# Seven block products in place of eight in a feed-forward block, and down projections in thirds

## The chip, the cores and the metric

The kernel runs on one core of one Trainium2 chip. The metric is the device time of one execution in microseconds (us): the median of 3 timed runs. A profile is of one further execution. TensorE (PE) multiplies, VectorE (DVE), ScalarE (ACT) and GpSimd (POOL) work elementwise, SyncE (SP) issues transfers. SBUF is the on-chip memory, PSUM the eight banks that PE writes to.

## The reference

Two layers of an encoder trunk, all in float32, for 512 prompt frames and 8 x 16 sample frames, 640 rows of 1024 together. A layer is

```
h = h + 0.5 * rmsnorm(swiglu(rmsnorm(h, g0), f1g, f1u, f1d), g1)
h = h + rmsnorm(mixer(rmsnorm(h, g2)), g3)
h = h + 0.5 * rmsnorm(swiglu(rmsnorm(h, g4), f2g, f2u, f2d), g5)
swiglu(x, wg, wu, wd) = (silu(x @ wg) * (x @ wu)) @ wd      # 1024 -> 2816 -> 1024
```

The mixer (pooling, sliding-window attention, a short convolution, three gates and an output projection) is not part of the change.

## The kernel before

Everything is transposed: features lie on the 128 partitions and frames along the free dimension, in two halves of `HT` = 320 frames. 1024 features are `KD` = 8 tiles, 2816 hidden features `NF` = 22 tiles. A float32 operand is split into a high part (rounded to float32r) and a low part (the rest), and each product is made in three passes, high x high, high x low, low x high, so one k-tile costs three matmuls of 128 x 128 by 320.

A *group* (`group`, line 529) is one output tile of 128 features by 320 frames in one PSUM bank: 24 matmuls with 8 k-tiles. A *pair* is two weight columns of 128 (slots 0 and 1) by two halves: four groups in banks 0 to 3. For a gate/up pair the two slots are the gate and the up column of one hidden tile f, so f costs 4 x 24 = 96 matmuls. SP loads the weights of a slot into `raw` in four transfers. ACT rounds them to `w_hi`, and DVE subtracts to get `w_lo` (both called `stage`, lines 851 and 1158). PE waits for `w_split` (weights ready) and `evac` (bank free), the second four groups back.

A feed-forward block (FFN), `ffn` on each engine, runs twice a layer, four times in all. It has two halves fg. Each has `FG` = 11 gate/up tiles, then the down projection over these 11 hidden tiles (four pairs, 33 matmuls a group); the second half adds to `y_ffn`. For each gate/up half-tile DVE takes `scaled` and `up` from PSUM times `inv_x` (line 1279), ACT applies silu, DVE multiplies to `mid` (line 1286), ACT rounds `mid_hi`, and POOL subtracts for `mid_lo` (line 1615). Before the first down group PE waits for `mid_split`:

```
pe.wait_ge(mid_split, unit + 2 * FG - 1)
...
for q in range(4):
    if q == 2:
        pe.wait_ge(mid_split, unit + 2 * FG)
```

A *seam* joins two blocks. While PE makes the last eight down groups (`last_four`) and the first eight groups of the next block (`first_four`, 2 weight pairs), the other engines finish the norm of the old block, update `h`, and make `x_hi`, `x_lo` of the next: squares on ACT, their sums on POOL (`add_square`, line 1577), column sums and spreading on PE (`sums`, `spread`), root on ACT, reciprocal and `new_h`, `x_low` on DVE. The order of the squares is written out in `SEAM_SQ` (behind an FFN) and `SEAM_SQ_MIX` (behind a mixer), and `first_four` places the sums differently behind a mixer. In the first tiles (`hidden_four`) the takes wait for `inv_x`.

The order of each engine is written by hand. Loops over layers, tiles and pairs run on the engines (`Fori`).

Of the kernel before, what the change touches and what calls it, by code (L numbers as in the profile page):

```python
# [8 lines left out]
F32R = mybir.dt.float32r  # L28
# [3 lines left out]
ds = bass.ds  # L32

P = 128
# [9 lines left out]
FG = NF // 2  # L44
# [12 lines left out]
FFN_PAIRS = 2 * (FG + KD // 2)  # L57
# [21 lines left out]
DVE_STEPS = 3 * 20 + 4 * ATT_STEPS + 5 + 2 * KD  # L79
POOL_STEPS = 3 * 4 + 3 + 8 + 2 + 6  # L80
# [7 lines left out]
           ("x", 5), ("y", 14), ("x", 6), ("x", 7), ("y", 15)]  # L88
SEAM_SQ_MIX = SEAM_SQ[:13] + [("y", 15), ("x", 6), ("x", 7)]


def trunk_kernel(nc, x_prompt, x_sample, state_pool, state_conv, cache_k, cache_v, norm_g, ffn1_w_gate,
# [5 lines left out]
    with ctx:  # L98
# [16 lines left out]
        at_h, at_x, at_mid, at_y = take(KD * TB), take(2 * KD * TB), take(24 * TB), take(KD * TB)  # L115
# [4 lines left out]
        mid_hi = view("mid_hi", FG * NT, at_mid, F32R)  # L120
        mid_lo = view("mid_lo", FG * NT, at_mid + FG * TB, F32R)
        br_hi = view("br_hi", KD * NT, at_mid, F32R)
        br_lo = view("br_lo", KD * NT, at_mid + KD * TB, F32R)
        mg_lo = view("mg_lo", KD * NT, at_mid + 2 * KD * TB, F32R)
        rows = view("rows", 5 * D, at_mid)
        in_mid = [at_mid + 2 * KD * TB]

        def in_mg(name, cols):
# [7 lines left out]
        assert in_mid[0] <= at_mid + 3 * KD * TB  # L136
        y_ffn = view("y_ffn", KD * NT, at_y)
        mg_hi = view("mg_hi", KD * NT, at_y, F32R)
# [6 lines left out]
        raw = [own(f"raw{s}", FG * P) for s in range(2)]  # L145
        w_hi = [own(f"w_hi{s}", FG * P, F32R) for s in range(2)]
        w_lo = [own(f"w_lo{s}", FG * P, F32R) for s in range(2)]

        W8 = 4 * KD * P
        w_first, w_out_last = (
            [[view(f"{n}_{part}{s}", KD * P, at_mid + off + W8 * (2 * s + i), F32R) for s in range(2)]
             for i, part in enumerate(("hi", "lo"))]
            for n, off in (("w_first", 16 * TB - 8 * W8), ("w_out_last", 16 * TB - 4 * W8)))
        assert 16 * TB - 8 * W8 >= 2 * TB and 8 * P <= 4 * 2 * P

        at_tmp = take(8 * 4 * HT + 256)
        scaled = [view(f"scaled{s}", HT, at_tmp + 4 * HT * s) for s in range(2)]
        silu = [view(f"silu{s}", HT, at_tmp + 4 * HT * (2 + s)) for s in range(2)]  # L160
        up = [view(f"up{s}", HT, at_tmp + 4 * HT * (4 + s)) for s in range(2)]
        mid = [view(f"mid{s}", HT, at_tmp + 4 * HT * (6 + s)) for s in range(2)]
        w_tail = view("w_tail", 4 * (FG - KD) * P, at_tmp, F32R)
        sig = [view(f"sig{s}", HT, at_tmp + 4 * HT * (2 + s)) for s in range(6)]
        PB = 4 * (WIN + 1) + 4
        prob = [view(f"prob{s}", PB, at_tmp + 4 * PB * s) for s in range(3)]
        prob_t = [view(f"prob_t{s}", 4 * P, at_tmp + 12 * PB + 16 * P * s) for s in range(2)]
        assert 12 * PB + 32 * P <= 8 * 4 * HT + 256

        at_seam = take(12 * 4 * HT)  # L170
        sq, diag, low, acc_y, acc_x, tb = (
            [view(f"{n}{s}", HT, at_seam + 4 * HT * (2 * i + s)) for s in range(2)]
            for i, n in enumerate(("sq", "diag", "low", "acc_y", "acc_x", "tb")))
        tb.append(own("tb2", HT))
        v_win = view("v_win", 8 * P, at_seam)
        win_v = view("win_v", PE_W, at_seam + 32 * P)
        assert 32 * P + 4 * PE_W <= 6 * 4 * HT
        inv_x = [own(f"inv_x{s}", HT) for s in range(2)]
        xv = [own(f"xv{s}", HT) for s in range(2)]
        k_s = own("k_s", DEC_B * KEYS_S)  # L180
        at_vs = take(4 * DEC_B * P)
        v_s = view("v_s", DEC_B * P, at_vs)
        pc_out = view("pc_out", 8 * P, at_vs)
        at_kr = take(16 * P)
        k_raw = view("k_raw", 4 * P, at_kr)
        prm_rows = view("prm_rows", DEPTH * P, at_kr)
        at_sr = take(4 * (PW + CW))
        sp_raw, sc_raw = view("sp_raw", PW, at_sr), view("sc_raw", CW, at_sr + 4 * PW)
        new_rows = view("new_rows", 4 * P, at_sr)
        kv_out = own("kv_out", 3 * P)  # L190
        wp = own("wp", DEPTH * 2 * P)
        wp_now = own("wp_now", 2 * P)
# [8 lines left out]
        eps1, eps4 = own("eps1", 1), own("eps4", 1)  # L201
# [16 lines left out]
        mid_made = sem("mid_made")  # L218
        mid_hi_made = sem("mid_hi_made")
# [78 lines left out]
        def w_cols(part, where, s, nk):  # L298


            if where == "main":
                return [(0, nk, (w_hi, w_lo)[part][s][:, 0:nk * P])]
            if where in ("first", "out_last"):
                return [(0, nk, (w_first if where == "first" else w_out_last)[part][s][:, 0:nk * P])]
            over_x = (x_hi, x_lo)[part][:, 4 * s * NT:4 * (s + 1) * NT].rearrange("p (k t) -> p k t", t=NT)
            o = (2 * s + part) * (FG - KD) * P
            return [(0, KD, over_x[:, :, HT:HT + 2 * P]), (KD, nk, w_tail[:, o:o + (nk - KD) * P])]

        def w_tile(part, where, s, k):
            if where == "x":  # L310
                if k < KD:
                    at = (4 * s + k // 2) * NT + HT + (k % 2) * P
                    return (x_hi, x_lo)[part][:, at:at + P]
                o = ((2 * s + part) * (FG - KD) + k - KD) * P
                return w_tail[:, o:o + P]
            return {"main": (w_hi, w_lo), "first": w_first, "out_last": w_out_last}[where][part][s][:, k * P:(k + 1) * P]

        def raw_cols(s, a, z, like):
            r = raw[s][:, a * P:z * P]
            return r.rearrange("p (k c) -> p k c", c=2 * P) if len(like.shape) == 3 else r  # L320
# [66 lines left out]
        def _(sp):  # L387
# [12 lines left out]
            def columns(w, l, row0, nk, col, slot):  # L400

                src = w[ds(l, 1)].rearrange("a (k p) c -> p (a k) c", p=P)[:, row0 // P:row0 // P + nk, :]
                dst = raw[slot][:, 0:nk * P].rearrange("p (k c) -> p k c", c=P)
                q = (nk + LOADS - 1) // LOADS
                return [(dst[:, a:min(a + q, nk)], src[:, a:min(a + q, nk), ds(col, P)]) for a in range(0, nk, q)]
# [27 lines left out]

            def ffn(n, l, first):
                for g in range(2):
                    pair = l * PAIRS + FFN_PAIR0[n] + (FG + KD // 2) * g

                    with sp.Fori(2 if first and g == 0 else 0, FG) as f:
                        gate_up(pair + f, n, l, f + g * FG)
                    with sp.Fori(0, KD // 2) as i:  # L440
                        for s in range(2):
                            load(pair + FG + i, s, columns(w_ffn[n][2], l, g * FG * P, FG, (2 * i + s) * P, s))
# [10 lines left out]
            with sp.Fori(0, DEPTH) as l:  # L453
# [62 lines left out]
        def _(pe):  # L516
# [28 lines left out]
            K8, KF = range(KD), range(FG)  # L545
# [5 lines left out]
            def first_four(pair, g, n, after_mixer):  # L551
# [5 lines left out]
                def stand(at):  # L557

                    if at == ((0, "lo", 0, 0) if after_mixer else (0, "hi", 1, 1)):
                        sums(acc_y[1], BY[1], sq0 + (22 if after_mixer else 24))  # L560
                    if at == ((0, "lo", 1, 2) if after_mixer else (0, "hi", 1, 4)):
                        sums(acc_x[0], BX[0], sq0 + 24)
                    if at == ((0, "all", 2, 0) if after_mixer else (0, "lo", 0, 1)):
                        spread(BY[1], 4 * n + 1)
                    if at == ((0, "all", 2, 4) if after_mixer else (0, "lo", 1, 0)):
                        spread(BX[0], 4 * n + 2)
# [1180 lines left out]
```

## Time and profile before

| | |
|---|---|
| median of the timed runs | 2792.03 us (2791.22 to 2793.0) |
| span of the profiled execution | 2795.9 us |
| mean granted clock of TensorE | 0.991 |
| busy PE, DVE, ACT, POOL | 2757.9, 1245.5, 849.1, 447.1 us |
| moved by transfers | 208.44 MB, mean 75 GB/s |

The span runs from the first to the last instruction of the profiled execution and is 3.9 us above the median of the timed runs. A busy time counts an engine's instructions; PE's matmuls are pipelined, so one lasts longer (0.31 us) than the distance to the next. A granted clock of 1.00 is 2.4 GHz, 0.50 is 1.2 GHz.

### The profile page before, as it was taken

How to read it: one execution, taken by the hardware profiler on the slowest of the kernel's cores; microseconds unless marked ns; L12 is line 12 of the kernel's file. 1: busy time of each engine (PE TensorE's matmuls, PEld its weight loads, DVE VectorE, ACT ScalarE, POOL GpSimd, SP SyncE). 2: the span in 40 equal slices, each digit the busy share in tenths (PEclk: the TensorE clock that was granted, in tenths of full speed). 3: DMA queues.
4: the chain of work that ended last, by engine and by line, in shares of the span. 5: the costliest groups of instructions: out<-in, count | busy, mean ns of one | idle time of the engine just before them, and what ended most of it. 6: DMA issues, size and time to landing. Idle time of an engine off the chain costs nothing.

```text
span 2795.9 us, 54256 instructions
## 1 busy us (share of the span) xinstructions
PE 2757.9 (99%) x18682; PEld 2719.4 (97%) x18682; DVE 1245.5 (45%) x1997; ACT 849.1 (30%) x1331; POOL 447.1 (16%) x473
## 2 busy tenths in 40 slices
PE   8999999999999999999999999999999999999998
PEld 8999999989999999999999999999899999999997
DVE  5332333674444733233453333355644455333335
ACT  4221223333333522122332122233333343212223
POOL 3100112240001410011321001132300032100112
PEclk9999999999999999999999999999999999999998
DMA  3232222122223222222222222221122222222222
GB/s 104 75 90 86 73 82 71 48 61 66 74 73 91 59 73 81 66 75 87 65 70 75 83 83 75 86 73 50 46 75 75 77 76 61 75 83 76 74 79 89
DMA packets 425146, 208.44 MB, mean 75 GB/s; under 512 B 42425, under 2 KB 423323, under 8 KB 424987
## 3 DMA queue, kind: packets, MB, share of 16 engines
q1 hardware_dynamic: 421956, 203.46, 25.3%
q10 hardware_dynamic: 3062, 3.38, 0.4%
q8 instruction: 68, 1.11, 0.2%
q14 instruction: 60, 0.48, 0.1%
HBM read 203.28 MB, written 5.29 MB: 75 GB/s over the span
## 4 chain that ended last, share of the span: by engine, by line
PE 94%; DVE 3%; issue 1%; ACT 0%; POOL 0%; DVEq 0%; DMA 0%; SPq 0%; ACTq 0%; POOLq 0%
PE ps L540 30%; PE ps L541 29%; PE ps L542 29%; DVE h L1198 1%; DVE x_lo L1180 1%; PE ps L593 1%; PE ps L641 1%; PE ps L588 1%; PE ps L589 1%; PE ps L663 1%; PE ps L521 1%; DVE w_lo L1162 0%; PE ps L527 0%; POOL acc_y L1580 0%; PE ps L691 0%
## 5 line engine op out<-in xcount | busy, mean ns | idle before, releaser
L540 PE MATMUL ps<-x_hi,w_hi 128*128 128x320 f32 x3648 | 1136.6, 312 | 0.0
L542 PE MATMUL ps<-x_hi,w_lo 128*128 128x320 f32 x3648 | 1127.2, 309 | 0.0
L541 PE MATMUL ps<-x_lo,w_hi 128*128 128x320 f32 x3648 | 1127.0, 309 | 0.0
L540 PEld LDWEIGHTS ps<-x_hi,w_hi 128*128 128x128 f32 x3648 | 684.8, 188 | 11.4 <-issue 6.5
L541 PEld LDWEIGHTS ps<-x_lo,w_hi 128*128 128x128 f32 x3648 | 685.0, 188 | 0.2
L542 PEld LDWEIGHTS ps<-x_hi,w_lo 128*128 128x128 f32 x3648 | 684.8, 188 | 0.0
L858 ACT ACTIVATE w_hi<-raw 128x1024 fp32r<-128x1024 f32 (+1 forms) x326 | 362.3, 1114 | 758.8 <-PE ps L542 758.8
L1162 DVE TENSOR_TENSOR w_lo<-raw,w_hi 128x1024 fp32r<-128x1024 f32 (+1 forms) x326 | 423.4, 1300 | 179.9 <-ACT w_hi L858 179.9
L540 PE MATMUL ps<-mid_hi,w_hi 128*128 128x320 f32 x1232 | 382.0, 310 | 0.0
L541 PE MATMUL ps<-mid_lo,w_hi 128*128 128x320 f32 x1232 | 380.7, 309 | 0.0
L542 PE MATMUL ps<-mid_hi,w_lo 128*128 128x320 f32 x1232 | 380.7, 309 | 0.0
L1615 POOL TENSOR_TENSOR mid_lo<-mid,mid_hi 128x320 f32 x160 | 141.1, 882 | 1297.6 <-ACT mid_hi L948 677.3
L1279 DVE TENSOR_TENSOR up<-ps,inv_x 128x320 f32<-128x320 f32 x176 | 86.3, 490 | 332.7 <-PE ps L542 332.7
L541 PEld LDWEIGHTS ps<-mid_lo,w_hi 128*128 128x128 f32 x1232 | 231.3, 188 | 0.3
L540 PEld LDWEIGHTS ps<-mid_hi,w_hi 128*128 128x128 f32 x1232 | 231.3, 188 | 0.3
L1580 POOL TENSOR_TENSOR acc_y<-acc_y,sq 128x320 f32<-128x320 f32 x96 | 113.3, 1180 | 739.5 <-ACT sq L869 739.2
L542 PEld LDWEIGHTS ps<-mid_hi,w_lo 128*128 128x128 f32 x1232 | 231.3, 188 | 0.0
L1279 DVE TENSOR_TENSOR scaled<-ps,inv_x 128x320 f32<-128x320 f32 x176 | 86.3, 490 | 247.3 <-PE ps L542 247.3
L948 ACT ACTIVATE mid_hi<-mid 128x320 f32 (+1 forms) x80 | 37.8, 472 | 316.9 <-DVE mid L1286 316.9
L1208 DVE COPY y_ffn<-ps 128x320 f32 (+1 forms) x64 | 31.5, 492 | 200.8 <-PE ps L542 200.8
L1337 DVE TENSOR_TENSOR scaled<-ps,inv_x 128x320 f32<-128x320 f32 x96 | 47.1, 491 | 163.5 <-PE ps L542 163.5
L1580 POOL TENSOR_TENSOR acc_x<-acc_x,sq 128x320 f32<-128x320 f32 x104 | 103.1, 991 | 91.6 <-ACT sq L869 72.8
(199 smaller groups left out, 3001.1 us busy)
## 6 DMA issues: line engine op xcount, KB each, us to landing
raw<-in_ffn_w_gate_dram SPq DMA_DIRECT2D x360, 128.0 KB, 2.2
raw<-in_ffn_w_up_dram SPq DMA_DIRECT2D x360, 128.0 KB, 2.3
raw<-in_w_in_dram SPq DMA_DIRECT2D x304, 128.0 KB, 2.2
raw<-in_ffn_w_down_dram SPq DMA_DIRECT2D x192, 192.0 KB, 2.7
raw<-in_ffn_w_down_dram SPq DMA_DIRECT2D x64, 128.0 KB, 2.8
raw<-in_w_branch_dram SPq DMA_DIRECT2D x64, 128.0 KB, 2.6
raw<-in_w_out_dram SPq DMA_DIRECT2D x64, 128.0 KB, 2.3
rows<-in_x_prompt_dram SPq DMA_DIRECT2D x4, 512.0 KB, 5.3
```

Source lines behind the costliest of these rows:

```text
L521: mm = pe.matmul(ps[0:SP_, b, c:c + 1], acc[:, c * SP_:(c + 1) * SP_], ones[:, 0:1], start=True, stop=True)
L540: pe.matmul(bank(b), wh, tile(xh, k, hf), start=k == ks[0], stop=False)
L541: pe.matmul(bank(b), wh, tile(xl, k, hf), start=False, stop=False)
L542: mm = pe.matmul(bank(b), wl, tile(xh, k, hf), start=False, stop=k == ks[-1])
L858: ins = act.activation(dst, raw_cols(s, a, z, dst), ACT.Copy)
L948: act.activation(at_tile(mid_hi, f, 0), mid[0][:, :], ACT.Copy).then_inc(mid_hi_made, 1)
L1162: ins = dve.tensor_tensor(lo, raw_cols(s, a, z, lo), f32(hi), ALU.subtract)
L1208: dve.tensor_copy(dst, bank(q)).then_inc(evac, 1)
L1279: dve.tensor_tensor(dst[:, :], bank(b), inv_x[hf][:, :], ALU.mult).then_inc(evac, 1)
L1337: return dve.tensor_tensor(dst, cut(bank(b), cols, bb), cut(inv_x[hf], cols, bb), ALU.mult)
L1580: pool.tensor_tensor(acc[:, :], acc[:, :], sq[pos % 2][:, :], ALU.add).then_inc(sq_added, 1)
L1615: pool.tensor_tensor(at_tile(mid_lo, f, hf), mid[hf][:, :], f32(at_tile(mid_hi, f, hf)), ALU.subtract).then_inc(mid_split, 1)
```

## The change

Of the 22 hidden tiles of an FFN the first 3 are made as before. The other 19 are made in runs of 3, 8 and 8 (`RUNS`), each run followed by a down projection over 6, 8 and 8 hidden tiles (`KT`).

For such a tile the four blocks of the activations (two halves of frames by two halves of four k-tiles) and the four blocks of the weights (two halves of k-tiles by gate and up) form a 2 x 2 product. It is made by Strassen's method in Winograd's form: 7 products of 4 k-tiles (`product`, 12 matmuls each) in place of 8. Needed beside them are four sums of weight blocks per tile (`sum_b`, 128 x 512 each, DVE), a high and a low part of seven weight blocks (`hi` on ACT, `low` on DVE, 128 x 512 each, in a ring of seven slots), four sums of activation blocks once an FFN (`so_sum`, `so_split`, `so_low`, 16 instructions of 128 x 320 each), and sums of the products in PSUM (DVE, 7 reads of PSUM a tile; ACT copies the first product to `p1s`). The low part of the hidden tile moves from POOL to DVE for these tiles. A tile's weights come in eight transfers (`pair_load`) into one of two buffers, one of which shares its place with `raw`.

```diff
@@ constants @@
-FG = NF // 2
+KT = (6, 8, 8)
+RUNS = ((3, 3), (6, 8), (14, 8))
+PRODUCTS, EVACS, SUMS_B = 7, 9, 4
...
@@ constants @@
-           ("x", 5), ("y", 14), ("x", 6), ("x", 7), ("y", 15)]
-SEAM_SQ_MIX = SEAM_SQ[:13] + [("y", 15), ("x", 6), ("x", 7)]
+           ("x", 5), ("y", 14), ("y", 15), ("x", 6), ("x", 7)]
...
@@ tensor: product @@
+            def product(S, i, b, x):
+                pe.wait_ge(s_split, PRODUCTS * S + i + 1)
+                for k in range(4):
+                    wh, wl = ring_w(i, 0, k), ring_w(i, 1, k)
+                    xh, xl = x(0, k), x(1, k)
+                    pe.matmul(bank(b), wh, xh, start=k == 0, stop=False)
+                    pe.matmul(bank(b), wh, xl, start=False, stop=False)
+                    mm = pe.matmul(bank(b), wl, xh, start=False, stop=k == 3)
+                mm.then_inc(s_prod, 1)
...
@@ tensor: strassen @@
+                product(S, 0, bank_free(0), lambda p, k: tile(xs[p], k, 0))
+                sums_ready(4)
+                product(S, 1, bank_free(1), lambda p, k: so_tile(sos[p], 0, k))
+                product(S, 2, bank_free(2), lambda p, k: tile(xs[p], 4 + k, 0))
+                sums_ready(S_OPS)
+                product(S, 3, bank_free(3), lambda p, k: tile(xs[p], k, 1))
+                product(S, 4, bank_free(4), lambda p, k: so_tile(sos[p], 1, k))
+                product(S, 5, bank_free(5), lambda p, k: tile(xs[p], 4 + k, 1))
+                product(S, 6, bank_free(6), lambda p, k: so_tile(sos[p], 2, k))
...
@@ tensor: ffn, before a down projection @@
+                    pe.wait_ge(mid_split, unit - 2)
+                    for q in range(4):
+                        pe.wait_ge(s_evac, EVACS * (S1 + 2) + TAKEN_BY[PRODUCTS - 4 + q])
+                        alone(pe)
+                        group(pd, gd + q, q % 2, q, (mid_hi, mid_lo), ks, q // 2, last_mid if q == 0 else None)
...
@@ scalar: ffn, per Strassen tile @@
+                        act.activation(p1s[:, :], bank(product_bank(t, PRODUCTS * r)), ACT.Copy).then_inc(p1_taken, 1)
+                        if r:
+                            strassen_mid(S - 1, f - 1, ft - 1, 0)
+                        if more:
+                            hi(S + 1, t, r + 1, 0)
+                            hi(S + 1, t, r + 1, 1)
+                        strassen_silu(S, 0)
+                        if more:
+                            for i in range(2, 6):
+                                hi(S + 1, t, r + 1, i)
+                            strassen_silu(S, 1)
+                            strassen_mid(S, f, ft, 1)
+                            hi(S + 1, t, r + 1, 6)
+                        else:
...
@@ vector: ffn, the three ordinary tiles @@
+                scale(scaled[0], 0, 0, g0)
+                scale(scaled[1], 2, 0, g0 + 2)
+                so_sum(0)
+                multiply(0, 1, g0 + 1)
+                multiply(1, 3, g0 + 3)
+                so_sum(1)
+                second_half(sm - 1)
+                scale(scaled[0], FIRST_BANKS[0], 1, g0 + 4)
+                stage(p0 + 2, 0, KD)
+                multiply(2, FIRST_BANKS[1], g0 + 5)
+                stage(p0 + 2, 1, KD)
+                so_sum(2)
+                so_sum(3)
+                so_low(0, 2)
+                scale(scaled[1], 2, 1, g0 + 6)
+                multiply(3, 3, g0 + 7)
+                so_low(1, 1)
+                S0 = s_base(l, n, 0)
+                front(S0, 0, 0)
+                scale(scaled[0], 0, 0, g0 + 8)
+                front(S0, 0, 1)
+                multiply(4, 1, g0 + 9)
+                so_low(2, 3)
+                front(S0, 0, 2)
+                scale(scaled[1], 2, 1, g0 + 10)
+                multiply(5, 3, g0 + 11)
+                so_low(3, 0)
...
@@ vector: ffn, per Strassen tile, behind two weight sums @@
+                        dve.tensor_tensor(p_u2[:, :], made(1), p1s[:, :], ALU.add).then_inc(s_evac, 1)
+                        if more:
+                            low(S + 1, r + 1, 0)
+                        dve.tensor_tensor(scaled[0][:, :], made(2), p1s[:, :], ALU.add).then_inc(s_evac, 1)
+                        if more:
+                            sum_b(S + 1, t, r + 1, 2)
+                        dve.wait_ge(s_evac, taken + 2)
+                        dve.tensor_tensor(scaled[0][:, :], scaled[0][:, :], inv_x[0][:, :], ALU.mult).then_inc(s_evac, 1)
+                        dve.wait_ge(s_evac, taken + 1)
+                        dve.tensor_tensor(p_u3[:, :], made(3), p_u2[:, :], ALU.add).then_inc(s_evac, 1)
+                        if more:
+                            low(S + 1, r + 1, 1)
...
@@ vector: ffn, last tile of a run @@
+                            stage(pd, 0, KT[t])
+                        dve.tensor_tensor(p_u2[:, :], made(6), p_u2[:, :], ALU.add).then_inc(s_evac, 1)
...
@@ vector: ffn, behind the last tile of a run @@
+                    stage(pd, 1, KT[t])
+                    mid_low(S, ft, 1)
+                    mid_low(S, ft, 0)
...
@@ tensor, and so on every engine @@
-            with pe.Fori(0, DEPTH) as l:
+            for l in range(DEPTH):
```

In the three ordinary tiles the up half is multiplied straight out of PSUM (`multiply`), without the scaling by `inv_x`. To allow this, POOL puts the norm's factor into the sum of squares behind the block (`begin(..., True)`). All seams use one order, the former one behind a mixer. The loop over the layers is written out on every engine.

## Rows read from the trace of the kernel before

**Rows 1.** The page's first part: busy us, share of the span, instructions.
```profile
PE 2757.9 (99%) x18682; PEld 2719.4 (97%) x18682; DVE 1245.5 (45%) x1997; ACT 849.1 (30%) x1331; POOL 447.1 (16%) x473
```
**Rows 2.** The page's chain that ended last, by engine.
```profile
PE 94%; DVE 3%; issue 1%; ACT 0%; POOL 0%; DVEq 0%; DMA 0%; SPq 0%; ACTq 0%; POOLq 0%
```
**Rows 3.** Windows: us, busy PE, PEld, DVE, ACT, POOL (x), clock, DMA, GB/s.
```profile
60.00:230.00 170.00, 170.00 (x1161) 170.00 (x1160) 59.65 (x86) 41.71 (x59) 16.75 (x19) 1.00 0.28 81
```
**Rows 4.** Timeline of DVE, a gate/up tile: start, us, instruction [idle before].
```profile
152.22 0.49 DVE L1279 TENSOR_TENSOR scaled<-ps,inv_x 128x320 f32<-128x320 f32 x1 [2.28 <-PE ps L542]
...
156.83 1.23 DVE L1162 TENSOR_TENSOR w_lo<-raw,w_hi 128x1024 fp32r<-128x1024 f32 x1 [0.60 <-ACT w_hi L858]
157.97 0.48 DVE L1286 TENSOR_TENSOR mid<-silu,up 128x320 f32<-128x320 f32 x1
...
166.30 0.49 DVE L1279 TENSOR_TENSOR scaled<-ps,inv_x 128x320 f32<-128x320 f32 x1 [2.27 <-PE ps L542]
```
**Rows 5.** Timeline of DVE, first takes of the FFN behind a mixer.
```profile
950.32 0.48 DVE L1279 TENSOR_TENSOR scaled<-ps,inv_x 128x320 f32<-128x320 f32 x1
950.72 0.48 DVE L1279 TENSOR_TENSOR up<-ps,inv_x 128x320 f32<-128x320 f32 x1
```
**Rows 6.** Groups by line and form on ACT: count, busy us, mean ns, idle before.
```profile
L858 ACT ACTIVATE w_hi<-raw 128x1024 fp32r<-128x1024 f32 x270 | 285.0, 1058 | 490.3 <-PE ps L542 490.3
...
L948 ACT ACTIVATE mid_hi<-mid 128x320 f32 x72 | 34.0, 472 | 286.3 <-DVE mid L1286 286.3
```
**Rows 7.** Timeline of SP, four transfers of a weight slot.
```profile
70.36 2.06 SPq L398 DMA_DIRECT2D raw<-in_ffn_w_gate_dram  x4
```
**Rows 8.** The page's DMA issues: count, KB each, us to landing.
```profile
raw<-in_ffn_w_gate_dram SPq DMA_DIRECT2D x360, 128.0 KB, 2.2
```
**Rows 9.** Timeline of DVE, low parts of activations in two seams.
```profile
944.15 5.64 DVE L1180 SCALAR_TENSOR_TENSOR x_lo<-h,prm,x_hi 128x320 fp32r<-128x320 f32 x8
...
1405.65 1.47 DVE L1180 SCALAR_TENSOR_TENSOR x_lo<-h,prm,x_hi 128x320 fp32r<-128x320 f32 x3
```
**Rows 10.** Timeline of POOL beside the first of these; beside the second it has none.
```profile
938.60 8.53 POOL L1580 TENSOR_TENSOR acc_x<-acc_x,sq 128x320 f32<-128x320 f32 x8 [8.73 <-ACT sq L869]
```
**Rows 11.** Timeline of ACT, first silu of the FFN behind a mixer.
```profile
953.05 0.47 ACT L962 ACTIVATE silu<-scaled 128x320 f32<-128x320 f32 x1
```
**Rows 12.** Timeline of DVE, takes at two seams, mixer to FFN and FFN to FFN.
```profile
908.09 0.49 DVE L1208 COPY y_mix<-ps 128x320 f32<-128x320 f32 x1 [3.03 <-PE ps L542]
...
962.75 0.49 DVE L1279 TENSOR_TENSOR scaled<-ps,inv_x 128x320 f32<-128x320 f32 x1 [0.58 <-PE ps L542]
...
1376.44 0.49 DVE L1206 TENSOR_TENSOR y_ffn<-ps,y_ffn 128x320 f32<-128x320 f32 x1 [4.35 <-PE ps L542]
...
1436.84 0.49 DVE L1279 TENSOR_TENSOR scaled<-ps,inv_x 128x320 f32<-128x320 f32 x1 [0.56 <-PE ps L542]
```
**Rows 13.** Timeline of PE in the seam from FFN to mixer.
```profile
500.48 1.23 PE L521 MATMUL ps<-ones,acc_y 128*80 128x1 f32 x8 [2.66 <-POOL acc_y L1580]
```
**Rows 14.** Windows in two seams, columns as in rows 3.
```profile
499.00:500.00 1.00, 0.00 (x0) 0.00 (x0) 0.66 (x2) 1.00 (x2) 0.44 (x1) 0.94 0.36 81
500.00:501.00 1.00, 0.52 (x4) 0.53 (x5) 0.62 (x1) 0.35 (x1) 0.42 (x1) 0.50 0.00 0
...
510.00:511.00 1.00, 1.00 (x6) 0.81 (x6) 0.97 (x3) 0.30 (x1) 0.00 (x0) 0.94 0.00 0
...
924.00:928.00 4.00, 2.28 (x14) 1.76 (x13) 4.00 (x6) 2.52 (x6) 3.36 (x4) 1.00 0.16 47
```
**Rows 15.** Timeline of PE in the seam from mixer to FFN.
```profile
925.93 0.41 PE L588 MATMUL ps<-x_hi,w_hi 128*128 128x320 f32 x1 [0.58 <-ACT x_hi L876]
...
927.62 0.41 PE L588 MATMUL ps<-x_hi,w_hi 128*128 128x320 f32 x1 [1.14 <-ACT x_hi L876]
```
**Rows 16.** Timeline of DVE: last up take, first down take of an FFN.
```profile
183.90 0.49 DVE L1279 TENSOR_TENSOR up<-ps,inv_x 128x320 f32<-128x320 f32 x1 [0.48 <-PE ps L542]
...
188.87 0.49 DVE L1208 COPY y_ffn<-ps 128x320 f32 x1 [1.53 <-PE ps L542]
```

More of the change, by code:

```diff
@@ L154, in trunk_kernel @@
+        assert 2 * TB + 3 * W8 <= 8 * TB
+        w_out_last, w_x = (
+            [[view(f"{n}_{part}{s}", KD * P, at + W8 * (2 * s + i), F32R) for s in range(2)]
              for i, part in enumerate(("hi", "lo"))]
[L155 to L158 removed]
+            for n, at in (("w_out_last", at_mid + 16 * TB - 4 * W8), ("w_x", at_s)))
@@ L165, in trunk_kernel @@
+        sig = [view(f"sig{s}", HT, at_tmp + 4 * HT * (2 + s) if s < 4 else at_free + 4 * HT * (s - 4)) for s in range(6)]
         PB = 4 * (WIN + 1) + 4
         prob = [view(f"prob{s}", PB, at_tmp + 4 * PB * s) for s in range(3)]
[L167 to L171, printed above, removed]
+        assert 12 * PB <= 6 * 4 * HT
@@ L309, in w_tile, with w_of @@
-        def w_tile(part, where, s, k):
[L310 to L320, printed above, removed]
+        def w_of(part, where, s):
+            return {"main": (w_hi, w_lo), "first": w_first, "out_last": w_out_last, "x": w_x}[where][part][s]
@@ new lines, in ffn @@
+                for k in range(4):
+                    act.wait_ge(h_ready, 16 * (sm + 1))
+                    alone(act)
+                    act.activation(so_tile(so_raw, 0, k), tile(h, 4 + k, 1), ACT.Copy,
+                                   scale=gcol(l, 4 * n, 4 + k)).then_inc(xgb_made, 1)
+                roots(BX[1], sm - 1, 3, False)
+                silu_of(0, 1)
+                silu_of(1, 2)
+                keep_inv_x(1, sm - 1)
+                mid_hi_of(0, 0, 0, 3)
+                mid_hi_of(1, 1, 0, 4)
@@ L1135, in _ @@
             roots(BX[0], -1, 2, False)
-            with act.Fori(0, DEPTH) as l:
+            for l in range(DEPTH):
                 ffn(0, l, 3 * l, l, 2)
@@ L1559, in _ @@
             inverse(-1, 2)
-            with dve.Fori(0, DEPTH) as l:
-                own_.loop(l, DVE_STEPS)
+            for l in range(DEPTH):
                 ffn(0, l, 3 * l, l, 2)
@@ L1700, in _ @@
                 add_square(acc_x[0], 0, 16 + j)
-            with pool.Fori(0, DEPTH) as l:
-                own_.loop(l, POOL_STEPS)
+            for l in range(DEPTH):
                 ffn(0, l, 3 * l)
```

631 lines of the change are left out of this document (410 added, 221 removed).

## The prediction

> **What bounds the kernel now.** I read the page's busy times first, then its chain, then one stretch by windows, then single instructions in the timeline. TensorE (PE) is busy for 99% of the span, VectorE, ScalarE and GpSimd for less than half of it [rows 1], and the chain that ended last is 94% PE [rows 2]. In the stretch from 60 to 230 us, all gate/up and down projection, PE has no idle time, its granted clock is 1.00 (2.4 GHz), and 1161 matmuls take 170 us, 146.4 ns each [rows 3]. The same period comes out of the loop: the take of one group recurs after 166.30 - 152.22 = 14.08 us for 96 matmuls, 146.7 ns each [rows 4]. Group boundaries are inside both figures, so a boundary costs nothing visible. A time that falls must come from fewer matmuls, and the question is what PE then waits for.
>
> **What it removes.** A tile of hidden columns is now eight block products of 4 k-tiles by 3 passes, 96 matmuls; as a Strassen tile it is seven, 84. 19 of 22 tiles of each feed-forward block (FFN) change, and there are four FFNs: 12 x 19 x 4 = 912 matmuls. The down projections keep theirs (16 groups x 22 tiles x 3, cut 6 + 8 + 8 instead of 11 + 11). 912 x 146.7 ns = **-133.8 us**. Products of 12 matmuls double the boundaries; at the boundary cost of rows 3 and 4 that is nothing.
>
> **The Strassen step, per tile.** PE needs 84 x 146.7 ns = 12.32 us, 1.76 a product. VectorE (DVE) gets a new load. Per tile it issues four weight sums and seven low parts of 128x512, seven reads of PSUM at 128x320, and six more at 128x320 (two scalings, two hidden products, two hidden low parts): 11 wide and 13 narrow. The trace has no 512-wide instruction of this kind, so its spacing lies between neighbours: narrow ones without a wait start 0.40 us apart although each lasts 0.48 [rows 5], and a 1024-wide one is followed after 157.97 - 156.83 = 1.14 us although it lasts 1.23 [rows 4]. On the line between them 512 costs 0.60. So DVE needs 11 x 0.60 + 13 x 0.40 = 11.8 us of 12.32, 96%. From above: if spacing were the whole duration (0.48; 0.69 on the line to 1.23), 11 x 0.69 + 13 x 0.48 = 13.8. From below a lighter DVE gives PE nothing, since PE bounds then. I take 11.8, since rows 4 and 5 are the same instruction shapes, and cost the step at PE's 12.32. The cover is thin, but a late DVE doesn't stop PE at once: the next tile's weights are split during this one, and a bank comes round after eight products. The dependent pairs have another instruction between them, which fills the result's latency. ScalarE (ACT) has seven roundings of 512, one copy, two silus and two roundings of 320; 1024 takes it 1.06 us and 320 takes 0.47 [rows 6], so 512 some 0.63: 7 x 0.63 + 5 x 0.47 = 6.8 us, half of the step. Its in-order waits could add to DVE's 11.8, which is a rival below.
>
> The Trainium skill, VectorE: DVE Perf Modes, section "The DRAIN you can't avoid", says that after each DVE instruction the pipe is flushed and the next cannot start before it is empty. Read as a spacing of the whole duration that speaks against this change, and it is the slower rival below; the trace's 0.40 after a 0.48 us instruction doesn't bear it out so far.
>
> Weight traffic stays 1 MB a tile in eight DMAs. Four are issued in 2.06 us [rows 7] and land after 2.2 [rows 8], so eight are in after about 2 x 2.1 + 2.2 = 6.4 us. A buffer comes free some 3 us into one step and is wanted 3 us into the next: 12 us. Hidden; if the cover were gone, the excess over 12 would be paid at each tile.
>
> GpSimd (POOL) loses the hidden low parts but for six a FFN. DVE's three-operand instructions take 5.64 us for eight while POOL adds squares and 1.47 for three when it doesn't [rows 9, 10], some 0.7 against 0.47 from one to the next, so DVE also runs undisturbed in the Strassen steps. I use undisturbed spacings there.
>
> **Entry into Strassen, once a FFN.** The three ordinary tiles now carry the sums of the activations: on DVE 12 sums at 0.47, 4 at 0.40, 16 low parts at 0.40, 12 takes and products at 0.40, two weight splits at 1.14, four weight sums and four lows at 0.60 up to the fourth product: 25.5 us. In the FFN after the mixer DVE is free for it at 950.3 [rows 5]. Added to it are round trips through ACT, which follow in order: silu before the first product (its table load ends at 953.05 [rows 11]), the rounding of the sums behind the rounding of the hidden tile, the silu of the third tile behind three weight roundings that themselves wait for a DVE sum. Laid out instruction by instruction they and POOL's interference cost DVE some 7.7 us. So the fourth product can start at 950.3 + 25.5 + 7.7 = 983.5. PE, undisturbed, would want it at: the ninth group ends at 962.75 [rows 12], so the seventh starts at 952.2; six groups of 3.52 and three products of 1.76 lead to 978.6. **4.9 us lost**, in three pieces (about 1.6 at the seventh group, whose bank now waits for a product behind four sums; 0.8 at the second Strassen product; 2.5 at the fourth).
>
> Idle PE can cost twice. After 2.66 us of idleness [rows 13] the granted clock was 0.50 (1.2 GHz) from about 499.9 until 510.9 [rows 14], some 5.5 us lost; after 0.58 and 1.14 us [rows 15] it stayed at 1.00 [rows 14]. A stall of 2.5 lies between, near the first; I take about half, 2.5 us. Entry: 4 x 7.4 = **+30**; bounds 0 (all round trips overlap) and 4 x (8 + 5.5) = 54.
>
> **Exit into the down projection, three times a FFN instead of twice.** Before, the first down group is read 188.87 - 183.90 = 4.97 us after the last up group, for 33 matmuls (4.84): 0.13 lost [rows 16]. After, the first down weights are split between two takes: that split starts 0.8 us before the last product ends, lasts 1.23 and releases PE 0.5 us late. The hidden low parts of the last tile come behind 0.35 + 3 x 0.40 + 1.14 + 0.40 + 0.49 = 3.6 us, which 21 matmuls (3.1 us) cover; with 6 tiles only 15 do, so 1.1 us is lost there and 0.55 at the other two. Per FFN 2.2 - 2 x 0.13 = 1.9, **+8** in all; bounds 0 and 3 x 4 x 3.6 = 43. Returning from down to Strassen costs nothing: banks 4 to 7 are free and the first three weight splits lie in the last down pair, where DVE has 14.08 us for about 9.
>
> **Seams.** The last eight down groups shrink from 11 tiles to 8, and the order of the seam becomes that of the one behind the mixer. From the first of these eight groups to the end of the next block's first eight, the mixer's seam takes 962.75 - 3.52 - (908.09 - 14.08) = 65.2 us for 384 matmuls (56.3), 8.9 over; that between two FFNs 1436.84 - 3.52 - (1376.44 - 19.36) = 76.2 for 456 (66.9), 9.3 over [rows 12]. So the shorter cover costs nothing: 0; bounds -8 and +8 over four seams. At the very end of the kernel no PE work follows, and some DVE work moves behind it; +1.
>
> **Sum.** Against the profiled execution: 2795.9 - 133.8 + 30 + 8 + 1 = 2701.1. The span lies 3.9 above the median of the timed runs, 2792.03, so the forecast is 2697 us, 3.4% faster.
>
> **Rivals.**
> - *DVE becomes the bound.* Place: every Strassen step but the last of a run. Price: DVE's spacing above 12.32. With whole durations, 13.8, 76 x 1.48 = 112 us are given back: 2809, slower. It decides from 12.32 + 95/76 = 13.6 us a tile. For: 24 instructions with up to three waits each. Against: rows 4 and 5. 8%.
> - *Waits between DVE and ACT stretch the step a little.* A weight rounding waits for a sum and the low part for the rounding: four handovers a tile that fit only just. 0.3 to 0.9 us a tile, 23 to 68 in all: 2720 to 2765, middle 2741. 20%.
> - *Entry and exit are hidden.* Then only the matmuls count: 2795.9 - 133.8 + 1 - 3.9 = 2659; with some exits left 2665. For: ACT has half its time free. 10%.
> - *The matmuls don't get cheaper by their number*, since shorter products open gaps. 532 more boundaries would need 0.18 us each to take the gain; rows 3 and 4 leave no room. 1%.
>
> **How the numbers follow.** Forecast 61%, from 2672 to 2720 (entry and exit between a third and one and a half times what I took, the seams within their bounds). With the rivals the range is 2662 to 2765: it leaves out the slower rival and the tails. A change of 0.2%, 5.6 us, is what a measurement can tell. Slower is the first rival and the worst of the others: 8%; within 0.2% only a DVE step near 13.6 us, 2%; faster 90%.
>
> **What would show it.** 912 matmuls fewer, at the same period; between Strassen products no idle PE, takes 12.3 us apart, and DVE over 90% busy there; idle PE of about 5 us around the third to seventh Strassen product group of each FFN, perhaps with a clock of 0.50 behind it; about 0.5 to 1 us at each of twelve exits. It is wrong if takes of the same product are 13 us or more apart (DVE or its handovers bound), if PE idles in the seams more than now, or if the clock falls inside the Strassen runs.

## The result, and the profile after

The changed kernel takes 2703.2 us (median of four runs) against 2792.5 for the kernel before on the same chip: ratio 0.9686, 95% interval 0.9672 to 0.9699, so 3.1% faster. One of its four runs, 2711.3 us, had a lower mean clock (0.989 against 0.993). The forecast was 2697 us, in a range from 2662 to 2765. The profiled execution spans 2701.7 us; the working had come to 2701.1 for it, before it took off the 3.9 us by which the median stood below the span then (now it stands 1.5 above).

The page's first part of the changed kernel, as in [rows 1]:

```profile
PE 2630.0 (97%) x17770; PEld 2580.8 (96%) x17770; DVE 1847.4 (68%) x3405; ACT 1032.0 (38%) x1891; POOL 322.8 (12%) x321
```

TensorE (PE) has 18682 - 17770 = 912 matmuls fewer. Busy time falls by 127.9 us rather than 133.8, and the time outside it rises from 38.0 to 71.7. Windows in a run of Strassen tiles show none of that, columns as in [rows 3]:

```profile
180.00:200.00 20.00, 20.00 (x139) 20.00 (x138) 19.72 (x40) 8.67 (x19) 0.00 (x0) 1.00 0.32 88
200.00:220.00 20.00, 20.00 (x138) 20.00 (x137) 19.44 (x40) 10.81 (x23) 0.00 (x0) 1.00 0.26 73
220.00:240.00 20.00, 20.00 (x139) 20.00 (x138) 19.55 (x39) 8.97 (x19) 0.00 (x0) 1.00 0.19 54
```

PE never stops there, at a clock of 1.00, and VectorE (DVE) is busy for 97 to 99%. The period is read from ScalarE's (ACT) timeline, the copy of each tile's first product:

```profile
170.10 0.42 ACT L1122 ACTIVATE p1s<-ps 128x320 f32<-128x320 f32 x1
...
182.42 0.42 ACT L1122 ACTIVATE p1s<-ps 128x320 f32<-128x320 f32 x1
```

182.42 - 170.10 = 12.32 us, the forecast period to the hundredth. What was lost stands in the waits of PE (releaser, us in total, times, longest):

```profile
PE ps L680 <- DVE ring L1494: 18.2, 8, 2.8
...
PE ps L599 <- DVE w_lo L1331: 5.6, 12, 0.6
PE ps L599 <- DVE mid L1441: 5.5, 4, 1.5
...
PE ps L599 <- DVE mid_lo L1544: 2.0, 4, 0.5
```

The first row is the entry (second and fourth product, four FFNs), the third the entry's seventh group, the second and the last are the exits. Each stop costs more than its row says. The timeline of PE at one exit, as start, us and instruction:

```profile
253.77 0.31 PE L682 MATMUL ps<-so_hi,ring 128*128 128x320 f32 x1
254.63 0.41 PE L599 MATMUL ps<-mid_hi,w_hi 128*128 128x320 f32 x1 [0.56 <-DVE w_lo L1331]
254.88 0.31 PE L600 MATMUL ps<-mid_lo,w_hi 128*128 128x320 f32 x1
```

Two steps of 0.147 us became 254.88 - 253.77 = 1.11, so 0.82 was lost where 0.56 is written as idle: a restart costs another 0.26, which the profile books as busy time. With 28 such stops at entries and exits (three and four an FFN) that is 7.3 us of busy time; busy time fell by 5.9 us less than the matmuls are worth.

Laid side by side by matmul, the two traces close. The table gives the time of PE in each stretch beyond 146.67 ns (14.08 us / 96) for every 128x320 product matmul in it, worked out from the PE timelines.

| Stretch | before | after |
|---|---|---|
| start of the span to the end of the first eight groups | 28.8 | 27.2 |
| FFN, from there to its last eight down groups, four FFNs | 0.0 | 8.6 + 8.6 + 8.6 + 11.3 = 37.0 |
| five seams, from a block's last eight groups to the end of the next block's first eight | 50.3 | 52.6 |
| the rest of the two mixers | 72.0 | 71.9 |
| end of the kernel | 25.7 | 27.8 |

The sum is +39.7 us; with 912 x 0.1467 = 133.8 less it is -94.1, and the spans differ by 94.2. The mixers' rest is the same in both, so nothing was lost or won there by writing out the loop over the layers; what that loop does elsewhere was not run by itself.

### The profile page after: what moved, and what is told of

It reads as the page before. It is cut to its first block and busy times, and to the rows that moved or that the text cites. A ratio compares the mean times of both kernels' runs of the same rounds, so it can differ in the third digit from the quotient of the medians.

```text
span 2701.7 us, 50293 instructions
## 1 busy us (share of the span) xinstructions
PE 2630.0 (97%) x17770; PEld 2580.8 (96%) x17770; DVE 1847.4 (68%) x3405; ACT 1032.0 (38%) x1891; POOL 322.8 (12%) x321
## 5 line engine op out<-in xcount | busy, mean ns | idle before, releaser
L1063 ACT ACTIVATE ring<-pair_raw 128x512 fp32r<-128x512 f32 x456 | 281.6, 622 | 460.1 <-DVE pair_raw L1485 329.0
L680 PE MATMUL ps<-x_hi,ring 128*128 128x320 f32 x1216 | 377.7, 311 | 9.7 <-DVE ring L1494 9.7
L599 PE MATMUL ps<-x_hi,w_hi 128*128 128x320 f32 x1216 | 385.3, 317 | 0.0
L681 PE MATMUL ps<-x_lo,ring 128*128 128x320 f32 x1216 | 377.2, 310 | 0.0
L682 PE MATMUL ps<-x_hi,ring 128*128 128x320 f32 x1216 | 377.1, 310 | 0.0
L601 PE MATMUL ps<-x_hi,w_lo 128*128 128x320 f32 x1216 | 376.0, 309 | 0.0
L600 PE MATMUL ps<-x_lo,w_hi 128*128 128x320 f32 x1216 | 375.9, 309 | 0.0
L1494 DVE TENSOR_TENSOR ring<-pair_raw,ring 128x512 fp32r<-128x512 f32 x456 | 298.4, 684 | 0.2
L680 PE MATMUL ps<-so_hi,ring 128*128 128x320 f32 x912 | 283.0, 310 | 8.5 <-DVE ring L1494 8.5
L681 PE MATMUL ps<-so_lo,ring 128*128 128x320 f32 x912 | 282.7, 310 | 0.0
L682 PE MATMUL ps<-so_hi,ring 128*128 128x320 f32 x912 | 282.7, 310 | 0.0
L599 PEld LDWEIGHTS ps<-x_hi,w_hi 128*128 128x128 f32 x1216 | 228.4, 188 | 11.2 <-issue 6.1
```

The costliest lines, as they stand in the source:

```text
L599: pe.matmul(bank(b), wh, tile(xh, k, hf), start=k == ks[0], stop=False)
L600: pe.matmul(bank(b), wh, tile(xl, k, hf), start=False, stop=False)
L601: mm = pe.matmul(bank(b), wl, tile(xh, k, hf), start=False, stop=k == ks[-1])
L680: pe.matmul(bank(b), wh, xh, start=k == 0, stop=False)
L681: pe.matmul(bank(b), wh, xl, start=False, stop=False)
L682: mm = pe.matmul(bank(b), wl, xh, start=False, stop=k == 3)
```

## The experiments

**1. The order at the entry.** At the entry of the second FFN, DVE stood idle six times, 5.9 us in all, though it was late. Its timeline in the changed kernel:

```profile
937.47 0.49 DVE L1441 TENSOR_TENSOR mid<-silu,ps 128x320 f32<-128x320 f32 x1 [0.59 <-issue]
938.94 2.12 DVE L1470 TENSOR_TENSOR so_lo<-so_raw,so_hi 128x320 fp32r<-128x320 f32 x4 [0.98 <-ACT so_hi L1053]
...
945.92 0.49 DVE L1441 TENSOR_TENSOR mid<-silu,ps 128x320 f32<-128x320 f32 x1 [1.74 <-ACT silu L1042]
947.40 2.11 DVE L1470 TENSOR_TENSOR so_lo<-so_raw,so_hi 128x320 fp32r<-128x320 f32 x4 [0.99 <-ACT so_hi L1053]
...
952.51 0.49 DVE L1441 TENSOR_TENSOR mid<-silu,ps 128x320 f32<-128x320 f32 x1 [0.59 <-issue]
953.98 2.11 DVE L1470 TENSOR_TENSOR x_lo<-so_raw,x_hi 128x320 fp32r<-128x320 f32 x4 [0.98 <-ACT x_hi L1053]
```

The longest, 1.74, is a silu that was ready to run and stood in ACT's queue behind two weight roundings, which waited for a sum of DVE. ACT's timeline:

```profile
944.32 1.15 ACT L1063 ACTIVATE ring<-pair_raw 128x512 fp32r<-128x512 f32 x2 [3.81 <-DVE pair_raw L1485]
945.38 0.46 ACT L1042 ACTIVATE silu<-scaled 128x320 f32<-128x320 f32 x1
```

The edit reorders both queues, with no instruction more or less:

```diff
@@ scalar @@
                 so_split(0, 1)
                 silu_of(3, 7)
-                mid_hi_of(3, 1, 1, 8)
                 so_split(1, 0)
+                so_split(2, 2)
+                mid_hi_of(3, 1, 1, 8)
...
-                for i in range(3):
-                    hi(S0, 0, 0, i)
+                hi(S0, 0, 0, 0)
                 silu_of(4, 9)
+                hi(S0, 0, 0, 1)
+                hi(S0, 0, 0, 2)
                 mid_hi_of(4, 2, 0, 10)
-                so_split(2, 2)
...
                 silu_of(5, 11)
-                mid_hi_of(5, 2, 1, 12)
                 act.wait_ge(group_done, g0 + 12)
                 so_split(3, 3)
+                mid_hi_of(5, 2, 1, 12)
@@ vector @@
-                so_sum(0)
+                so_sum(0, range(0, 1))
                 multiply(0, 1, g0 + 1)
                 multiply(1, 3, g0 + 3)
+                so_sum(0, range(1, 4))
                 so_sum(1)
...
                 stage(p0 + 2, 1, KD)
+                scale(scaled[1], 2, 1, g0 + 6)
                 so_sum(2)
                 so_sum(3)
-                so_low(0, 2)
-                scale(scaled[1], 2, 1, g0 + 6)
                 multiply(3, 3, g0 + 7)
+                so_low(0, 2)
                 so_low(1, 1)
...
-                front(S0, 0, 2)
                 scale(scaled[1], 2, 1, g0 + 10)
+                front(S0, 0, 2)
                 multiply(5, 3, g0 + 11)
```

> The changed kernel with nothing but the order of work at the entry into Strassen altered, on VectorE (DVE) and ScalarE (ACT): no instruction more or less. Theory A, order: at each entry DVE stands idle for 0.59 + 0.98 + 1.74 + 0.99 + 0.59 + 0.98 = 5.9 us in round trips through ACT, while its work alone, some 27 us from the first take, fits into the 26.4 us that TensorE (PE) has up to the fourth product, nearly. The changed kernel loses about 7 us of PE time per entry (6.4 us of idleness, three restarts) and some 5 us of clock in all. Then at most 2 us per entry stay: 2703 - 20 to 28 = 2675 to 2683 us. Theory B, amount: the number of sums, low parts and splits and GpSimd's interference set the entry; reordering moves the idle time of PE from one product to another: 2696 to 2705 us.

Measured: 2676.0 us, ratio 0.9575 (0.9562 to 0.9588). Theory A holds. PE's waits after the edit have one row left of the entry:

```profile
PE ps L599 <- DVE w_lo L1332: 5.6, 12, 0.6
...
PE ps L599 <- DVE mid_lo L1546: 2.0, 4, 0.5
...
PE ps L680 <- DVE ring L1495: 0.7, 1, 0.7
```

Of 23.8 us idle at the entries 0.7 are left, and the span falls by 27.5 us, since the restarts and the lost clock go too. DVE's timeline shows no idle time from 905 to 948 us, so its work does just fit.

**2. The first weight split at the exits.** One DVE instruction is moved:

```diff
+                        if not more:
+                            stage(pd, 0, KT[t])
                         dve.tensor_tensor(p_u3[:, :], made(5), p_u3[:, :], ALU.add)
...
-                        else:
-                            stage(pd, 0, KT[t])
```

> The changed kernel with one instruction moved: in the last tile of a run DVE splits the first down weights ahead of the take of the sixth product instead of behind it and the scaling that follows. Theory A: at the exits PE waits 0.29, 0.56 and 0.55 us for this split, each with a restart of 0.26 us, and DVE is idle for 0.87 us just before the sixth product; the split takes 1.22 us, so it ends ahead of the last product. The two exits with 8 tiles become free, the one with 6 tiles keeps its wait for the hidden low part (0.50 us), which comes up to 0.4 us later: gain (0.82 + 0.81 + 0.55 - 0.4) x 4 = 7 us, 2696 us (2694 to 2699). Theory B: what is late is the whole chain of takes behind the last product, and the wait turns up at the hidden low part instead: 2700 to 2705 us.

Measured: 2699.6 us, ratio 0.9665 (0.9652 to 0.9679). By its interval it can't be told from the changed kernel; the trace tells more. The waits for the split are gone, and others have come in their place:

```profile
PE ps L599 <- DVE mid_lo L1544: 6.5, 12, 0.9
```

5.6 + 2.0 us in 16 stops became 6.5 in 12; with restarts that is 11.8 - 9.6 = 2.2 us. Counted by matmul as in the table, the third FFN, where the clock fell in neither kernel, loses 7.7 us where it lost 8.6, and four times that is 3.6. The gain is a third to a half of A's 7, and the shift to the hidden low part that B named is real: DVE makes it behind the second weight split. Both theories were partly right.

**3. One and three more instructions a tile.** Each takes the short time of a 128x320 instruction and makes nothing that is used. The kernel with three puts one ahead of `low` 0, 2 and 3 each:

```diff
+            def one_more():
...
+                dve.tensor_tensor(tb[2][:, :], h[:, 0:HT], h[:, HT:2 * HT], ALU.subtract).then_inc(more_made, 1)
...
+                            one_more()
                             low(S + 1, r + 1, 2)
```

> The changed kernel with one more DVE instruction of 128x320 in each Strassen tile that is followed by another (64 in all), subtracting two parts of h into a spare tile. Theory A, PE bounds the tile and DVE has a slack of 0.27 us of idleness and 0.1 to 0.2 us of delayed starts in 12.32: the instruction takes 0.40, so nothing or up to 0.1 us a tile is added: 2703 to 2710 us. Theory B, the handovers between DVE and ACT already fit exactly, so that each instruction put between them is paid in full: 0.40 x 64 = 26 us, 2729 us.

Measured: 2703.7 us, ratio 0.9673 (0.9658 to 0.9688): nothing, as in A. Handovers that are paid in full would have cost 26 us.

> The same with three more DVE instructions of 128x320 in each of these tiles. Theory A: DVE then needs 11.8 + 1.2 = 13.0 us against PE's 12.32 and becomes the bound; by the slack of 0.4 us that the trace shows, (1.2 - 0.4) x 64 = 51 us are added: 2754 us (2740 to 2765), and takes of one product are 13.1 us apart. Theory B, handovers: 1.2 x 64 = 77 us, 2780 us. If DVE's instructions could overlap further (more slack than the trace shows): under 2735 us.

Measured: 2738.7 us, ratio 0.9806 (0.9791 to 0.9821): 35 us more, less than either theory. The period is as A said, from ACT's timeline of this kernel:

```profile
185.88 0.42 ACT L1123 ACTIVATE p1s<-ps 128x320 f32<-128x320 f32 x1
...
199.00 0.42 ACT L1123 ACTIVATE p1s<-ps 128x320 f32<-128x320 f32 x1
```

13.12 us; 11 x 0.60 + 16 x 0.40 = 13.0. DVE is the bound, and yet PE still runs at its own pace in the middle of the run (windows):

```profile
200.00:220.00 20.00, 20.00 (x138) 20.00 (x137) 20.00 (x43) 8.17 (x18) 0.00 (x0) 1.00 0.39 106
```

The debt is paid at the end of the run. PE's timeline, and one row of its waits:

```profile
249.83 0.39 PE L681 MATMUL ps<-x_hi,ring 128*128 128x320 f32 x1 [0.41 <-DVE ring L1501]
...
259.57 0.61 PE L600 MATMUL ps<-mid_hi,w_hi 128*128 128x320 f32 x1 [2.42 <-DVE w_lo L1338]
...
PE ps L600 <- DVE w_lo L1338: 24.3, 12, 3.6
```

Seven tiles at 0.8 us make 5.6 us of lag; PE is stopped for 0.41 + 2.42, of which 0.56 was there before. The other 3.3 us do not reach PE; that weights split a tile ahead and free banks swallow them is argued from the program, not shown. At the other ends of runs of eight the second stop lasts 2.39 to 3.61 us, so such a run forgives 2 to 3 us. The run of three has 1.6 us of lag: in the first FFN it forgives all of it (a stop of 0.29 us as before), in the others all but some 0.45 (0.74 to 0.77). So A failed in its price. Of the 35 us, 20.4 are idle time of PE at entries and exits (44.2 for 23.8). The mean clock also fell, to 0.989 from 0.993; 0.004 of 2735 us makes 11, an estimate.

**4. Entry and exits together.** On top of experiments 1 and 2:

```diff
@@ scalar, last tile of a run @@
-                            act.wait_ge(s_prod, PRODUCTS * (S + 1) + 5)
+                            act.wait_ge(s_prod, PRODUCTS * (S + 1) + 4)
                             stage(pd, 0, KT[t], None)
...
-                            act.wait_ge(s_prod, PRODUCTS * (S + 1) + 7)
+                            act.wait_ge(s_prod, PRODUCTS * (S + 1) + 6)
                             stage(pd, 1, KT[t], None)
@@ vector @@
-                    stage(pd, 1, KT[t])
+                    if t == 0:
+                        stage(pd, 1, KT[t])
                     mid_low(S, ft, 1)
                     mid_low(S, ft, 0)
+                    if t:
+                        stage(pd, 1, KT[t])
```

> The changed kernel with the new order at the entry and three edits at the exits: DVE splits the first down weights ahead of the sixth product's take; ACT rounds the two first weight slots one product earlier (as soon as the ring slot that it overwrites has been read); and in the runs of 8 tiles DVE makes the last hidden low parts ahead of the second weight split. The entry alone gave 2676 us. Moving the first split alone gave 3.6 us instead of 7, as the wait moved to the hidden low part (0.34 us at the exits with 8 tiles, 0.95 at the one with 6). Theory A, order again: at the exits with 8 tiles both the low parts (ready 0.9 us earlier) and the second split (wanted 3.5 us after the first) come in time, the one with 6 tiles keeps some 1.2 us with its restart: exits 11.8 us -> 5 us in all, 2669 us (2666 to 2672). Theory B: with the low parts first, the second split is late by what was won, so that the exit stays at the 8 us of the first edit: 2672 to 2675 us.

Measured: 2670.3 us, ratio 0.9555 (0.9542 to 0.9568), the fastest of all here: 4.45% under the kernel before. The exits are left with one row of waits, that of the six-tile third:

```profile
PE ps L599 <- DVE mid_lo L1546: 3.8, 4, 0.9
```

With its restarts that is 3.8 + 4 x 0.26 = 4.8 us, theory A's 5. The intervals of this kernel and of experiment 1 overlap, so the time alone does not prove the 5.8 us between them; the spans differ by 2.7.

**5. The hidden low parts on GpSimd (POOL).** Two DVE instructions a tile go to POOL:

```diff
@@ vector @@
-                            mid_low(S - 1, ft - 1, 1)
-                            mid_low(S - 1, ft - 1, 0)
...
-                    mid_low(S, ft, 1)
-                    mid_low(S, ft, 0)
@@ gpsimd, per Strassen tile, hf in (1, 0) @@
+                            pool.wait_ge(mid_hi_made, unit_of(l, n, f0 + r) + (1 if hf else 2))
...
+                            pool.tensor_tensor(tile(mid_lo, ft, hf), mid[0 if hf else 1][:, :], f32(tile(mid_hi, ft, hf)),
+                                               ALU.subtract).then_inc(mid_split, 1)
```

> The changed kernel with the hidden low parts of the Strassen tiles on GpSimd (POOL) instead of DVE, as the kernel before had them: two instructions of 128x320 a tile, 0.88 us each on POOL undisturbed. Theory A, PE bounds the tile: DVE loses 2 x 0.40 of work and gains interference while POOL works (0.47 -> 0.7 from one to the next of three-operand instructions in the seams, at most a third of 1.8 us a tile): no change inside the runs; at the exits the last low part no longer stands behind the second weight split on DVE, so the 0.50 us wait of the exit with 6 tiles may go: 2698 to 2705 us. Theory B, POOL's interference costs DVE more than it saves: DVE's step grows over 12.32 + 0.4, and the lag is paid at the end of each run as in the kernel with three more instructions: 2715 us or more.

Measured: 2716.6 us, ratio 0.9723 (0.9708 to 0.9738), 13 us slower: theory B's number (2715 or more), but not by its mechanism. The two engines do hold each other up. DVE's timeline, three low parts that take 1.89 us without POOL, in two tiles:

```profile
219.59 3.26 DVE L1494 TENSOR_TENSOR ring<-pair_raw,ring 128x512 fp32r<-128x512 f32 x3
...
232.20 1.89 DVE L1494 TENSOR_TENSOR ring<-pair_raw,ring 128x512 fp32r<-128x512 f32 x3
...
234.73 1.26 DVE L1481 TENSOR_TENSOR pair_raw<-pair_raw 128x512 f32<-128x512 f32 x1
```

and POOL's beside it:

```profile
219.94 2.36 POOL L1912 TENSOR_TENSOR mid_lo<-mid,mid_hi 128x320 fp32r<-128x320 f32 x2 [8.15 <-ACT mid_hi L1068]
...
232.55 4.17 POOL L1912 TENSOR_TENSOR mid_lo<-mid,mid_hi 128x320 fp32r<-128x320 f32 x2 [10.25 <-ACT mid_hi L1068]
```

In the first tile DVE pays 1.37 us, more than the 0.80 that it saved; 15 of the 64 tiles with a successor are like it. In the second it pays 0.57 at one weight sum (1.26 for 0.69), and POOL's pair takes 4.17 us instead; 38 of 76 pairs are like it. Averaged over the 76 pairs, the DVE instructions beside a pair last 0.57 us longer in sum than the median of their kind, less than the 0.80. So DVE does not fall behind, and B's lag does not show: PE stays busy through the runs, and its wait for the first down weights is 6.0 us in 12 stops, hardly more than 5.6. The time is lost at the exits, because POOL itself is late with the last low part. PE's waits:

```profile
PE ps L599 <- POOL mid_lo L1912: 10.1, 12, 1.2
```

(10.1 + 12 x 0.26) - (2.0 + 4 x 0.26) = 10.2 us, beside 10.5 between the spans. Smaller terms lie on both sides: 1.5 us less idle time at the entries, and a mean clock of 0.992 for 0.993.

**6. The seam's order alone, in the kernel before.**

```diff
-                for what, j in SEAM_SQ_MIX if nk == KD else SEAM_SQ:
+                for what, j in SEAM_SQ_MIX:
...
-                        first_four(pair, g, seam, n == 1)
+                        first_four(pair, g, seam, True)
...
@@ vector, seam (two places) @@
-                if nk == KD:
+                if True:
@@ gpsimd, behind an FFN @@
-                seam(sm, SEAM_SQ)
+                seam(sm, SEAM_SQ_MIX)
```

> The kernel before with nothing changed but the order of the seams behind an FFN, which becomes that behind the mixer (last take ahead of all low parts, sums and spreads of the norm one group later, last squares reordered). Theory A, the order decides: the seam from FFN to mixer lost 13.3 and 9.2 us of PE time in the kernel before and loses 9.8 and 8.8 in the changed one, the seam between FFNs 9.5 and 9.2 (without its seventh-group wait), the seam behind the mixer is untouched: gain 4 us, 2788 us (2785 to 2791). Theory B, the seams do not depend on it and what differs is where the clock happened to fall: 2791 to 2795 us, the same as before.

Measured: 2789.0 us, ratio 0.9982 (0.9972 to 0.9991), 5 us faster: theory A. Counted as in the table, PE loses 7.8, 8.3 and 7.8 us in the three seams behind an FFN, where it lost 12.3, 9.4 and 9.5 (the expectation's 13.3 and 9.2 end at different matmuls). In the first of these the clock, 0.50 at 500 us in [rows 14], stays up; the windows of this kernel:

```profile
486.00:502.00 16.00, 15.67 (x108) 14.57 (x108) 14.51 (x23) 7.04 (x15) 6.58 (x7) 1.00 0.25 55
502.00:518.00 16.00, 15.46 (x101) 14.23 (x101) 15.76 (x30) 8.16 (x18) 9.63 (x17) 1.00 0.29 65
```

Theory B has a share in it: before, the clock fell in all three of these seams, and now in none. But that is no accident of single executions: the mean clock is 0.996 in all ten of them, and at most 0.994 in the fifteen of the kernel before. PE's idle time in these seams falls from 8.2 to 4.0 us, as the stops of 2.66 and 2.69 us before the first sums are gone. So the order decides, in part through the clock.

## Why the prediction was right, point by point

| Step | forecast | measured |
|---|---|---|
| 912 matmuls | -133.8 | -133.8 |
| Strassen step at PE's 12.32 us | 0 | 0 |
| entry, four FFNs | +30 | +31.8 |
| exits | +8 | +11.8 |
| seams | 0 | -2.8 |
| start of the kernel | not priced | -3.1 |
| end of the kernel | +1 | +2.1 |

The terms of the forecast miss by +1.8, +3.8, -2.8, -3.1 and +1.1 us, and nearly cancel; that the sum came within 0.6 us of the span is luck, and the range is what the working could claim. The 3.9 us taken off at the end was misread as well: each profiled execution's own time lies some 2 us above its span (2797.7 for the 2795.9 of the rows), so that execution of the kernel before lay 4 to 5 us above the kernel's median.

**Matmuls and step.** Right to the digit, and for the reason given. DVE's spacing of a 128x512 instruction, estimated at 0.60 on a line between two neighbours, is 0.60: in the trace three of them last 1.89 us in all, 2 x 0.60 + 0.69. The step where DVE bounds, 13.1 us for 27 instructions, confirms it. So the rival of whole durations, 13.8 us for 24 instructions, is out: the next instruction starts 0.08 us before the recorded end of the last one. The prediction had it beside a rule of the Trainium skill (VectorE: DVE Perf Modes, "The DRAIN you can't avoid"), by which the next instruction waits for the pipe to empty. The same section adds that a next instruction that is not held starts earlier, which the prediction left out; the 0.08 us agree with that. The rival of stretched handovers is out by experiment 3. The rival of dearer boundaries counts 532 more of them, but 532 is the number of products; they replace 304 groups, so there are 228 more, and the 12.32 us a tile show no loss at them. A step at 96% of DVE was thin, and the prediction was right that a late DVE does not stop PE at once, but it priced its rival without that, as theory A of experiment 3 did: that kernel paid 35 us, not 51.

**Entry.** The sum is right, its pieces are not. Idle time at the seventh group was 1.44 us (forecast 1.6), at the second product 2.12 (0.8), at the fourth 2.82 (2.5); in the first FFN the seventh group waited 1.22 and the fourth product 1.29. That is 23.8 us in all instead of 19.6: the second product was under-sized, since the silu behind the weight roundings, which the prediction names, holds up everything behind it on DVE by 1.74 us, and the weight low part that this product needs is there. Restarts, which the prediction did not have, add 3.1. The clock was priced at 10 us, by the seam at 500 us (5.5 there, read a little long: 0.94 in the window from 510 puts its return to 1.00 at 510.1, so 5.1). Here 4.9 are left for it, since it fell at two entries of four. In the first FFN it fell after the second product's stop, and the fourth product then waited 1.5 us less, so this FFN lost 8.6 us in all, like the second and third, where it did not fall. In the fourth FFN it cost 2.7 us on top. The stops before look the same; PE's timeline of the second and of the fourth FFN:

```profile
956.83 0.38 PE L680 MATMUL ps<-x_hi,ring 128*128 128x320 f32 x1 [2.82 <-DVE ring L1494]
...
2284.17 0.60 PE L680 MATMUL ps<-x_hi,ring 128*128 128x320 f32 x1 [2.82 <-DVE ring L1494]
```

and the windows behind them:

```profile
958.00:960.00 2.00, 2.00 (x16) 2.00 (x15) 1.97 (x4) 0.00 (x0) 0.00 (x0) 1.00 0.10 30
...
2286.00:2288.00 2.00, 2.00 (x9) 2.00 (x8) 1.97 (x4) 0.00 (x0) 0.00 (x0) 0.50 0.38 111
```

One stays at 2.4 GHz, the other falls to 1.2. Why, no run here settles. Experiment 1 shows that the order of the two queues, and not the amount of work, cost the entry. The rival of hidden entries and exits did not come about in the changed kernel, but 2670 us shows that it was within reach of another order.

**Exits.** Idle time was 0.29 + 0.50 + 0.56 + 0.55 = 1.9 us an FFN; the forecast had 2.2, in the same places. For the exit with 6 tiles it said 1.1, where its own terms (3.6 us less 15 matmuls, 2.2) give 1.4; measured are 0.29 and 0.50. The term is under-sized by the restarts, 4 x 0.26 an FFN, and by the 0.13 a piece that was taken off for the kernel before: by matmul its exits lost nothing.

**Seams.** The step was priced at nothing and gave 2.8 us back: the order matters, worth 5 us in the kernel before by experiment 6. The prediction compared lengths of two seams (8.9 and 9.3) and left out the seam from FFN to mixer, although the rows at 500 us lay on the table. That the start got 3.1 us shorter may be the clock again (0.50 for 14 us before, for 3 after). In experiment 6 it was 7 us, and the start 3.6 us shorter than before, so the order of the first sums seems to have a part in it; neither was tested by itself. The end was 1 us worse than thought.

The entry's 31.8 us are the FFN stretch of the table less the exits, 37.0 - 11.8, plus the stops at the seventh groups, 5.6 + 4 x 0.26, which lie in the seams and in the start and are taken out of both.

## What to carry to other kernels

When an engine that was half idle gets close to the bound's pace, sum its instructions by start-to-start spacing, not by duration; then look at the ends of each run, where a lag of several tiles is paid at once. A stop at a transition can be no lack of time but an instruction that is ready and stands in an in-order queue behind one that is not: print that queue with its waits before buying slack. Count a restart with each stop: four stops of 0.5 us cost three quarters of a microsecond each.

## What the runs showed of the hardware

- A stop of PE costs 0.26 us beyond the idle time shown (254.63 above), which the profile counts as busy time.
- POOL beside DVE: POOL instructions of 128x320 that take 0.88 us each at the end of the changed kernel's entry took 2.36 and 4.17 us a pair in Strassen tiles of experiment 5, and DVE's three of 128x512 took 3.26 for 1.89 in 15 tiles of 64. The Trainium skill (SBUF — State Buffer, "SBUF: two separate sides") calls the port pair of the two engines an exclusive lock, which one holds for its whole instruction; by that rule, an estimate, DVE's three would take up to 1.89 + 2 x 0.88 = 3.65, and the trace's 3.26 does not contradict it.
- At idle times of the same length, 2.82 us, PE's clock fell in one FFN and not in another.
